# Short attention: where the two maps of a head are combined

## The reference

```python
def attend(args):
    qb, q0 = args
    s = jnp.einsum('bqhmd,bkhmd->bhmqk', qb, k, preferred_element_type=f32)
    ...
    s = s - slopes[None, :, None, None, None] * dist
    pr = jax.nn.softmax(s, axis=-1)
    att = pr[:, :, 0] - lam * pr[:, :, 1]
    return jnp.einsum('bhqk,bkhe->bqhe', att.astype(v.dtype), v)
```

## Time and profile before

| | |
|---|---|
| median of 3 runs | 3166.6 us (3165.26 to 3167.28) |
| the profiled execution, its own time | 3164.75 us |
| its span in the trace | 3163.0 us |
| busy in the span | PE 97%, DVE 73%, ACT 46%, POOL 26% |
| short stage, first scores to last sum | 1918.57 to 1974.75 us of the span |
| long stage, first scores | 1978.50 us |

### The profile page before, as it was taken

How to read it: one execution, slowest core, us unless ns; L and a number is a source line. 1 busy time by engine, 2 the same in 40 slices (tenths; PEclk the granted TensorE clock), 3 DMA queues, 4 the chain that set the end, 5 groups by cost and what they waited for, 6 DMA issues and landing times. The chain is left out here.

```text
span 3163.0 us, 67330 instructions
## 1 busy us (share of the span) xinstructions
PE 3054.4 (97%) x26625; PEld 2065.9 (65%) x26625; DVE 2320.4 (73%) x4206; ACT 1467.9 (46%) x3409; POOL 827.7 (26%) x1147
## 2 busy tenths in 40 slices
PE   7999999999999999899999988999999989999998
PEld 6888888544444444499999985677777744444444
DVE  4676675589999999277777767888888968854444
ACT  3555555444443544444444424677777722213322
POOL 0332333310000000133333311344444422222211
PEclk9999999999999999899999998999999999999999
DMA  4434443731414513565555557100000165521211
GB/s 170 160 113 161 153 134 126 268 137 55 131 53 120 155 48 90 146 194 182 154 153 154 158 165 233 57 15 22 15 19 19 68 245 176 175 92 60 90 60 44
DMA packets 312297, 377.45 MB, mean 119 GB/s; under 512 B 121756, under 2 KB 233832, under 8 KB 309552
## 3 DMA queue, kind: packets, MB, share of 16 engines
q1 hardware_dynamic: 295920, 361.38, 35.9%
q10 hardware_dynamic: 16064, 11.77, 1.2%
HBM read 205.31 MB, written 167.77 MB: 118 GB/s over the span
## 5 line engine op out<-in xcount | busy, mean ns | idle before, releaser
L2100 PE MATMUL at_g<-at_kT,at_qz 64*128 64x512 f32 x1088 | 285.7, 611 | 14.8 <-PEq L44 9.5
L2126 PE MATMUL at_pb<-at_v,at_attT 64*128 64x128 f32 x4352 | 282.6, 277 | 5.9 <-ACT at_o L1984 2.7
L658 PE MATMUL cv_pj<-u_room,w 128*128 128x257 f32 x1248 | 280.2, 384 | 2.0 <-DVEq L491 1.1
L658 PEld LDWEIGHTS cv_pj<-u_room,w 128*128 128x128 f32 x1248 | 237.2, 191 | 46.6 <-issue 12.0
L2126 PEld LDWEIGHTS at_pb<-at_v,at_attT 64*128 64x128 f32 x4352 | 261.3, 188 | 7.8 <-issue 7.6
L1083 PE MATMUL rs_tm<-w,rs_uT 128*128 128x512 f32 x480 | 207.7, 592 | 0.0
L1976 ACT COPY at_attT<-at_tb 128x512 f32<-128x512 f32 (+1 forms) x288 | 146.7, 561 | 109.2 <-PE at_tb L2112 109.2
L1023 DVE TENSOR_TENSOR rs_tmp<-rs_tt,u_room 128x63 f32<-128x63 f32 (+20 forms) x189 | 169.7, 898 | 27.0 <-POOL rs_tt L907 21.3
L1083 PE MATMUL rs_tm<-w,x_pair 128*128 128x512 f32 x416 | 183.0, 600 | 6.5 <-PEq L44 6.5
L658 PE MATMUL cv_pj<-cv_uT,w 128*128 128x257 f32 x832 | 183.5, 379 | 0.0
L1025 DVE TENSOR_TENSOR rs_tt<-rs_tt,rs_tmp 128x63 f32<-128x63 f32 (+20 forms) x189 | 173.3, 917 | 6.5
(11 more groups left out here) (378 smaller groups left out, 7189.8 us busy)
## 6 DMA issues: line engine op xcount, KB each, us to landing
scratch_packs<-pack_room SPq DMA_DIRECT2D x19, 2048.0 KB, 6.7
pack_room<-scratch_packs SPq DMA_DIRECT2D x54, 640.0 KB, 4.4
un_pk<-scratch_packs SPq DMA_DIRECT2D x25, 640.0 KB, 4.3
w<-in_w_in_dram SPq DMA_DIRECT2D x6, 2048.0 KB, 14.3
scratch_gate<-rs_tok_out SPq DMA_DIRECT2D x40, 256.0 KB, 2.6
scratch_local<-un_local_out SPq DMA_DIRECT2D x80, 128.0 KB, 2.0
at_v<-scratch_gate SPq DMA_DIRECT2D x20, 512.0 KB, 6.2
fn_xh<-in_x_dram SPq DMA_DIRECT2D x10, 1024.0 KB, 5.0
```

Of the source, the lines that this page charges most:

```text
L658: last = nc.tensor.matmul(pj[n % 3][0:r, 0:HALF], w[:, c, m * P:m * P + r], uT[b % 2][:, c, HALF * hf:HALF * hf + HALF], start=(c == 0), s ...
L2100: nc.tensor.matmul(gb[m][:, c * 512:(c + 1) * 512], qz[n % 2][rows, h, :], kT[rows, h, at:at + 512], start=True, stop=True).then_inc(s["sc ...
L2126: last = nc.tensor.matmul(pb[i][:, 0:P], attT[g % 2][rows, c, :], v[rows, c, h * P:(h + 1) * P], start=(c == 0), stop=(c == count - 1))
```

## The change

`SHARED` becomes 0 in the short stage. GpSimd then makes the whole combine of each of the 16 heads: 16 times the multiply and 16 times the add, on 128x512 tiles. VectorE keeps the reciprocal and the factor and loses its 16 combine instructions. The three engines that waited for `att_done` in the short stage (GpSimd before its multiply, VectorE before it writes `sc1` again, TensorE before it transposes) wait for `att_step` (the factor) and for `att_pool` (the add) instead. In the long stage every instruction and wait stays.

```diff
-    SHARED = 1024 if R == 2 else S
+    SHARED = 1024 if R == 2 else 0
...
                 pool.wait_ge(s["att_step"], 2 * g + 2)
-                pool.wait_ge(s["att_done"], g + 1)
+                if SHARED:
+                    pool.wait_ge(s["att_done"], g + 1)
                 nc.gpsimd.tensor_scalar(sc1[i][:, SHARED:S], sc1[i][:, SHARED:S], cf[:, i:i + 1], 1.0, ALU.mult, ALU.mult).then_inc(s["att_pool"], 1)
                 pool.wait_ge(s["att_pool"], 2 * g + 1)
                 nc.gpsimd.tensor_tensor(sc0[h][:, SHARED:S], sc0[h][:, SHARED:S], sc1[i][:, SHARED:S], ALU.add).then_inc(s["att_pool"], 1)
...
                     if g >= 2:
-                        dve.wait_ge(s["att_done"], g - 1)
+                        if SHARED:
+                            dve.wait_ge(s["att_done"], g - 1)
                         if SHARED < S:
                             dve.wait_ge(s["att_pool"], 2 * (g - 1))
...
-                part = slice(BR * P * r, BR * P * r + BR * P)
-                nc.vector.scalar_tensor_tensor(sc0[h][:, part], sc1[i][:, part], cf[:, i:i + 1], sc0[h][:, part], ALU.mult, ALU.add).then_inc(s["att_done"], 1)
+                part = slice(0, SHARED)
+                if SHARED:
+                    nc.vector.scalar_tensor_tensor(sc0[h][:, part], sc1[i][:, part], cf[:, i:i + 1], sc0[h][:, part], ALU.mult, ALU.add).then_inc(s["att_done"], 1)
...
             def turn(g, r):
-                if r == 0:
+                if r == 0 and SHARED:
                     pe.wait_ge(s["att_done"], g + 1)
-                else:
+                if r == R - 1:
                     pe.wait_ge(s["att_pool"], 2 * g + 2)
```

## The result

The changed kernel takes 3183.82 us (median of 6 runs, 3180.34 to 3185.03) and the kernel before 3166.94 us (6 runs, 3164.70 to 3170.13): a ratio of 1.0053 with a 95% interval of 1.0043 to 1.0063. The change makes the kernel 16.9 us slower. 3184.6 was forecast, with a range of 3179 to 3193.

A forecast was written before the change was run, and what follows sets the result against it. VectorE was taken to set the short stage's pace before, a closed VectorE-GpSimd chain after. Start 1.4, intervals 11.7, clock 1.0, contention 1.75 and end 2.3 make +18 us on 3166.6: 3184.6 us, range 3179 to 3193.

The forecast's parts named there:

- What is queued behind the new wait: VectorE's reduce of head g + 2 waits for GpSimd's add of head g; the next factor queues behind, closing a chain.
- The second rival: Short stage: the wait is hidden, as if the factor stood ahead of the reduce; no change, about 3165 us; chance 0.03.
- The chain of 3.87 us: Short stage, per head: GpSimd's add, VectorE's reduce and factor, GpSimd's combine, one after another; 3.87 us, bounds 3.76 to 3.96.
- The pair: GpSimd's multiply and add of 128x512 for each head, with the gap between: 1.92 us, bounds 1.81 and 2.01.
- The handovers: On the chain: GpSimd's add to VectorE's waiting reduce, 0.13 us, and VectorE's result to GpSimd's multiply, 0.18 us.
- Twice as slow: The Trainium skill's factor for two-input GpSimd operations: combine 1.50 us, total about 3179 us; the prediction kept 1.92 instead.
- The sum: Short stage: start 1.4, thirteen intervals 11.7, clock 1.0, contention 1.75 and end 2.3 give +18 us, bounds 13 and 23.
- Contention: Last two blocks: a distance-table piece on VectorE lengthens GpSimd's pair, 0.35 us in five intervals, +1.75 us (0 to 3.4).
- The clock at the start: TensorE enters the short stage at 1.2 GHz; one or two heads may go at its pace, +1.0 us (0 to 3).
- End: From the last reduce to the end of the last sum: 10.9 us instead of 8.6, +2.3 us (1.7 to 2.8).
- The third rival, the clock: Short stage: idle TensorE falls to 1.2 GHz repeatedly, 5.4 us a head instead of 3.87; 3195 to 3205 us; chance 0.10.
- What the profile after would show: Short stage: reduce idle 1 to 2 us, reduces 3.8 to 4.2 us apart, multiply 0.56 to 0.65, add 1.17 to 1.28.

The follow-up runs named there:

- after: The changed kernel (whole combine of the short stage on GpSimd) as profiled, against the kernel before: profiled execution 3180.34 us, median 3183.82 us, ratio 1.0053.
- scores first: Changed kernel with a third second-map tile and, on TensorE in the short stage, scores of head g + 3 ahead of head g's transposes: 3198.12 us, ratio 1.0103.
- factor first: Changed kernel with VectorE making the factor of head g + 1 before the reduce of head g + 2 in the short stage: 3172.07 us, ratio 1.0017.
- half the columns: Changed kernel with VectorE combining columns 0 to 255 of the short stage and GpSimd the rest: 3177.68 us, ratio 1.0034.

## Why the prediction was right

- **What is queued behind the new wait** was the step on which all depended, and it held. In after, reduce and multiply wait for each other; with the two instructions of the factor ahead of the wait, and nothing else changed, the intervals drop from 3.82 to 3.0. The second rival described that order and named about 3165 us for it. Its kernel took 3172: the rival had taken TensorE's 2.68 us or GpSimd's 2.5 for the next limit and missed the loop through ScalarE's exponentials.
- **The chain of 3.87 us** was 3.82, but two terms were off and cancelled, which is luck. The pair was taken at 1.92 and measured 2.04, outside its upper bound of 2.01. The failing term is the multiply: 0.60 taken, 0.65 as a bound, 0.69 to 0.70 measured. I took it between half of the 1.12 us of 1024 columns and what the add's scaling makes of them, and between 256 and 512 columns it is nearly flat, which the add is not. The handovers were taken at 0.31 in sum and measured 0.14. The add's end was followed by the reduce after 0.13 us in the long stage and after 0.04 here; in the first two heads of after it is 0.13 as well (1929.28 + 1.26 to 1930.67). Why it differs stays open.
- **Twice as slow.** The pair is 2.04 us where VectorE's combine took 0.75, 2.7 times. The Trainium skill's GPSIMD Engine Reference, section Engine selection, with its factor of about two gives an estimate of 1.50; the measurement decides, and the rows, with two instructions in place of one, were nearer.
- **The sum.** Thirteen intervals at 3.82 make 49.7 us, +11.0 over before (forecast 11.7). Contention was taken at 5 x 0.35 = 1.75 and was 5 x 0.29 = 1.45. In the interval of 4.24 it is the piece and not the add that is late, as shown above. The clock at the start was taken at 1.0 and was 0.55 (the interval of 4.37, where the reduce waits for scores at half clock). The clock did not rise about as soon as before: its mean is 0.71 in the stretch from 1934 to 1936, so it rose some 16.5 us after the stage's first reduce, against some 13 us in the kernel before (0.55 in 1932 to 1934). The later fall, for which the sum had no term, cost 0.13, and the interval of 3.92 has 0.10 more by its longer handover. Start +1.45 for +1.4. End +2.6 for +2.3: the last add ended 6.50 us after the last reduce (1978.61 to 1985.11; 6.3 to 6.6 forecast), and 4.74 instead of 4.3 us followed, with TensorE partly at 1.2 GHz. Stage +17.3 for +18.2, medians +16.9.
- **Contention** was right in size by a choice between 0 and 0.67. With the one-after-the-other of the rows above it could have been worked out: a piece of 0.67 that starts 0.2 us after the multiply ends some 0.5 us after it, and the add waits for the rest.
- **The third rival, the clock,** was right in kind. TensorE did fall to 1.2 GHz, once among the heads and once at the end. Its price was wrong: it priced a head at 5.4 us of TensorE's work, but the ring passes VectorE and GpSimd only, and TensorE at half clock, one head long, fits beside it but for 0.13 us. The rival's 1.2 us of idle time was in fact 1.35 us in one piece ahead of the transposes, and 1.64 in the last two blocks. The run with scores first, where the ring does pass TensorE, shows the price that the rival feared: 6.61 us.
- **What the profile after would show**: idle time of the reduce 1.79 and 1.15 us (1 to 2 forecast), reduces 3.8 to 4.2 us apart but for one of 4.37 and one of 4.24, a granted clock of 0.98 from 1934 to 1962 us and of 0.91 from there to 1980, later stages as long as before. The multiply fell outside what was written, and the last sum came 15.1 us later in the span and not some 18, since the stage began 2.2 us earlier in that execution.

## What to carry to other kernels

Before moving work to an idle engine, list what stands behind each new wait in every in-order queue, and go round until you are back: a ring of queues costs the sum of its members, however idle each engine is. Let short instructions that another engine waits for go ahead of a wait that they don't need, and check that this closes no new ring. Price an operation for another engine from its own rows at two sizes, not by scaling another operation.

## What the runs showed of the hardware

- GpSimd's multiply by a factor per partition hardly depends on size between 256 and 512 columns: 0.65 us for 128x256 (one instruction), 0.69 for 128x512, 1.12 for 128x1024. Its add does: 0.72, 1.26, 2.37.
- A table piece on VectorE (two inputs in SBUF) and an instruction on GpSimd run one after the other: piece 0.67 alone, 1.01 begun during a multiply, 1.59 and 1.70 begun during an add, ending 0.52 to 0.54 us after GpSimd's each time. The factor of the last head, a column of 128x1 that is begun during an add of after, takes 0.96 us instead of 0.22 (1981.74) and ends with that add. VectorE's reduce, which reads one of its inputs from PSUM, doesn't do this: in factor first it starts 0.06 us ahead of a multiply, and both keep their lengths (0.69 and 0.70).
- From the end of GpSimd's add in the profile to VectorE's waiting reduce it is 0.03 to 0.04 us in most heads of after, and 0.13 in its first two, in the long stage and in half the columns. A sum of GpSimd that is queued behind the add is not the reason: it stands there in half the columns too, and TensorE, which waits for the same add in after, starts 0.05 to 0.06 us after it with a sum behind it and without.
